# Inverting triangular blocks: four 32x32 blocks by powers and transposes, in place of two 64x64 blocks by squares

## The reference

```
h = rms_norm(x);  z = h @ w_in                      # 1024 -> q, k, v, gates of both branches
A: gated delta rule, 8 heads of 128, causal conv over 4 rows and SiLU on q, k, v
B: windowed attention, 16 heads of 64 on 2 key heads, window 128, sinks, relative bias
x + (sigmoid(gA) * (oa @ w_o_a) + sigmoid(gB) * (ob @ w_o_b)) @ w_out, then rms_norm
```

```
t_mat = eye + n_mat; p_mat = n_mat
for _ in range(5):                                  # chunks of 64
    p_mat = p_mat @ p_mat
    t_mat = t_mat + t_mat @ p_mat
```

## Time and profile before

| | |
|---|---|
| median of 3 runs | 2711.65 us |
| the profiled execution, its own time | 2707.76 us |
| its span | 2706.0 us |
| TensorE busy, matmuls | 2682.5 us, 99% |
| VectorE busy | 1416.5 us, 52% |
| ScalarE busy | 971.0 us, 36% |
| DMA, mean | 169 GB/s |

### The profile page before, as it was taken

One profiled execution on the slowest core, in us unless ns is written; L12 is line 12 of the kernel. 1 busy time (PEld: TensorE's weight loads), 2 busy tenths in 40 slices (PEclk: granted clock), 3 DMA queues, 4 the chain that ended last, 5 costly groups with the idle time before them and its releaser, 6 DMA issues.

```text
span 2706.0 us, 50329 instructions
## 1 busy us (share of the span) xinstructions
PE 2682.5 (99%) x19808; PEld 2274.0 (84%) x19808; DVE 1416.5 (52%) x3633; ACT 971.0 (36%) x3158; POOL 398.7 (15%) x238
## 2 busy tenths in 40 slices
PE   7999999999999999999999999999999999999998
PEld 6888888888888888888888888888888888888887
DVE  6777777233366666612236666651224666665012
ACT  4555455422244444421124444442112444444101
POOL 4333333443100110000000110000000011000000
PEclk9999999999999999999999999999999999999999
DMA  7554554787733333255453333335546333333564
GB/s 249 201 180 167 182 193 170 264 288 279 253 121 111 128 128 117 107 203 217 172 219 130 112 114 125 130 110 203 216 172 220 113 118 128 123 112 125 183 222 171
DMA packets 79001, 458.43 MB, mean 169 GB/s; under 512 B 13232, under 2 KB 17456, under 8 KB 31792
## 3 DMA queue, kind: packets, MB, share of 16 engines
q1 hardware_dynamic: 65664, 427.85, 44.2%
q10 hardware_dynamic: 13104, 27.36, 3.0%
HBM read 352.42 MB, written 102.76 MB: 168 GB/s over the span
## 4 chain that ended last, share of the span: by engine, by line
PE 96%; DMA 2%; POOL 1%; DVE 1%; ACT 0%; issue 0%; POOLq 0%; SPq 0%; ACTq 0%; DVEq 0%
PE bank L1305 24%; PE bank L1307 23%; PE bank L1306 23%; PE bank L1450 2%; PE last_banks L1450 2%; PE last_banks L1415 2%; PE bank L1434 2%; PE last_banks L1434 2%; PE bank L1403 2%; PE bank L1499 1%; PE bank L1491 1%; PE bank L1475 1%; PE last_banks L1557 1%; PE bank L1483 1%; PE bank L1548 1%; PE bank L1538 1%
## 5 line engine op out<-in xcount | busy, mean ns | idle before, releaser
L1305 PE MATMUL bank<-hT_hi,w_sl 128*128 128x512 f32 x2112 | 872.8, 413 | 0.0
L1307 PE MATMUL bank<-hT_hi,w_sl 128*128 128x512 f32 x2112 | 827.3, 392 | 0.0
L1306 PE MATMUL bank<-hT_lo,w_sl 128*128 128x512 f32 x2112 | 825.5, 391 | 0.0
L1307 PEld LDWEIGHTS bank<-hT_hi,w_sl 128*128 128x128 f32 x2112 | 396.7, 188 | 86.1
L1305 PEld LDWEIGHTS bank<-hT_hi,w_sl 128*128 128x128 f32 x2112 | 398.3, 189 | 71.6 <-issue 0.7
L1306 PEld LDWEIGHTS bank<-hT_lo,w_sl 128*128 128x128 f32 x2112 | 398.8, 189 | 65.4 <-issue 0.7
L436 POOL TENSOR_TENSOR w_sl<-w_raw,w_sl 128x1024 fp32r<-128x1024 f32 x90 | 218.3, 2430 | 391.2 <-ACT w_sl L517 381.6
L982 DVE SCALAR_TENSOR_TENSOR area<-zraw,stc,area 128x512 f32<-128x512 f32 x288 | 220.2, 765 | 4.2
L1148 DVE SCALAR_TENSOR_TENSOR s_cur<-s_cur,scs,last_banks 128x128 f32<-128x128 f32 x112 | 38.9, 348 | 199.8 <-PE last_banks L1554 199.8
L611 ACT ACTIVATE area<-area 128x512 f32<-128x512 f32 x96 | 60.4, 629 | 219.6 <-DVE area L982 219.6
L455 POOL TENSOR_TENSOR gu<-mk,g_hi 128x512 fp32r<-128x512 f32 x32 | 41.9, 1309 | 643.7 <-DVE nmx L1102 603.8
(11 more groups left out here) (244 smaller groups left out, 4817.7 us busy)
## 6 DMA issues: line engine op xcount, KB each, us to landing
w_sl<-saved_w SPq DMA_DIRECT2D x270, 1024.0 KB, 4.8
saved_w<-w_sl SPq DMA_DIRECT2D x90, 1024.0 KB, 4.9
w_raw<-in_w_tiles SPq DMA_DIRECT2D x90, 512.0 KB, 5.9
area<-in_x ACTq DMA_DIRECT2D x4, 2048.0 KB, 10.4
area<-in_x ACTq DMA_DIRECT2D x14, 512.0 KB, 8.1
out_y<-area ACTq DMA_DIRECT2D x3, 2048.0 KB, 8.1
bias_sb<-in_bias ACTq DMA_DIRECT2D x32, 128.0 KB, 2.3
out_y<-area SPq DMA_DIRECT2D x4, 512.0 KB, 2.7
```

The source lines that it names most:

```text
L1305: pe.matmul(dst, a_hi, b_hi, start=first, stop=False)
L1306: pe.matmul(dst, a_hi, b_lo, start=False, stop=False)
L1307: return pe.matmul(dst, a_lo, b_hi, start=False, stop=last)
```

## The change

The diagonal blocks are now of 32x32, four per tile (`BLOCKS`), and the levels are four. The stationary power is no longer made by a square on TensorE. The moving operand is the transposed power and the sum side by side (`fu_blk`, 64 columns per tile); the product gives the next transposed power, and VectorE's transpose of 32x32 blocks turns that into the next stationary power `p_blk`. There is one group of four tiles in place of two groups of two, so 16 matmuls in each apply. Behind each apply stands one fill, and the transposes of the probabilities stand behind the first. The 32x32 blocks are joined to 64x64 by two more products (`inner_in`, `inner_out`), with a copy by ScalarE between them and two by VectorE behind. The second logits are now in one piece between `inner_out` and `merge_in`. The rest of the corner is as it was. The diff, without renamed semaphores' declarations:

```diff
-LEVELS = 5
-LAST = 2 ** LEVELS
+BL = 32
+LEVELS = 4
+        BLOCKS = tuple(slice(r, r + BL) for r in range(0, P, BL))
+        CORNERS = ((BLOCKS[0], BLOCKS[1]), (BLOCKS[2], BLOCKS[3]))
-        p_sb = [blocks(area2[:, 4 * TB:4 * TB + NT * CH]), blocks(area2[:, 4 * TB + NT * CH:5 * TB])]
-        z_sb = p_sb[0]
+        z_sb = blocks(area2[:, 4 * TB:4 * TB + NT * CH])
+        inner = blocks(area2[:, 4 * TB + NT * CH:5 * TB])
+        yt, vt = inner[:, :, 0:BL], inner[:, :, BL:2 * BL]
+        f_blk, u_blk, fu_blk, p_blk = ptt[:, :, 0:BL], ptt[:, :, BL:2 * BL], ptt[:, :, 0:2 * BL], ptt[:, :, 2 * BL:3 * BL]
...
ScalarE
-                for lo, hi in HALVES:
-                    ins = act.activation(ptt[lo:hi, :, 0:CH], tt[lo:hi, :, lo:hi], ACT.Copy)
+                for r in BLOCKS:
+                    ins = act.activation(f_blk[r], tt[r, :, r], ACT.Copy)
                 ins.then_inc(pt0_ready, 1)
-                for lo, hi in HALVES:
-                    act.activation(p_sb[0][lo:hi], bch(5)[lo:hi, :, lo:hi], ACT.Copy)
...
-                for l in range(1, LEVELS + 1):
-                    p_copy(l, 0)
-                    p_copy(l, 1)
                 fill(1)
+                act.wait_ge(merge_product, merges(n1, 1))
+                act.activation(yt, bch(5)[:, :, 0:BL], ACT.Copy).then_inc(merge_act, 1)
...
VectorE
+            dve.tensor_reduce(stacked[:, :], mk[:, IDENT, :].rearrange("p (a c) -> p c a", c=BL), AX, ALU.add).then_inc(dve_init, 1)
...
-                for lo, hi in HALVES:
-                    ins = dve.tensor_tensor(ptt[lo:hi, :, CH:P], tt[lo:hi, :, lo:hi],
-                                            mk[lo:hi, IDENT:IDENT + 1, lo:hi].to_broadcast([CH, NT, CH]), ALU.add)
+                def first_powers():
+                    dve.wait_ge(pt0_ready, n1)
+                    dve.transpose(p_blk, f_blk)
+                    dve.tensor_tensor(u_blk, f_blk, stacked[:, None, :].to_broadcast([P, NT, BL]), ALU.add).then_inc(powers_ready, 1)
+                def level(l):
+                    dve.wait_ge(powers_done, powers(n1, l))
+                    dve.transpose(p_blk, bch(6)[:, :, 0:BL])
                     if l < LEVELS:
+                        ins = copy(f_blk, bch(6)[:, :, 0:BL])
                     if l > 1:
+                        dve.wait_ge(powers_ready, powers(n1, l))
+                        ins = dve.tensor_tensor(u_blk, bch(6)[:, :, BL:2 * BL], u_blk, ALU.add)
+                    ins.then_inc(powers_ready, 1)
                 def diagonal():
+                    dve.wait_ge(powers_ready, powers(n1, LEVELS + 1))
+                    dve.wait_ge(powers_done, powers(n1, LEVELS + 1))
+                    ch.link(dve.tensor_tensor(u_blk, bch(6)[:, :, BL:2 * BL], u_blk, ALU.add))
+                    dve.transpose(vt, u_blk).then_inc(merge_dve, 1)
+                    for r in BLOCKS:
+                        ins = copy(tt[r, :, r], u_blk[r])
                     ins.then_inc(diag_ready, 1)
+                def inner_corners():
+                    dve.wait_ge(merge_product, merges(n1, 2))
+                    for a, c in CORNERS:
+                        ins = copy(tt[a, :, c], bch(7)[a, :, 0:BL])
+                    ins.then_inc(merge_dve, 1)
...
                 logits(0)
+                first_powers()
                 attention()
                 fill(1)
                 quotient(0)
-                fill(2)
-                for l in range(1, LEVELS + 1):
-                    level(l, 0)
-                    level(l, 1)
-                settled()
+                fill(1)
+                level(1)
+                fill(1)
+                for l in range(2, LEVELS + 1):
+                    level(l)
                 diagonal()
+                inner_corners()
...
TensorE
+                def apply(l):
+                    c0, c1 = (0 if l <= LEVELS else BL), (2 * BL if l > 1 else BL)
+                    pe.wait_ge(powers_ready, powers(n1, l))
+                    for t in range(NT):
+                        for r in BLOCKS:
+                            ins = pe.matmul(bch(6)[r, t, c0:c1], p_blk[r, t, :], fu_blk[r, t, c0:c1], start=True, stop=True)
+                    ins.then_inc(powers_done, 1)
+                def inner_in():
+                    pe.wait_ge(merge_dve, merges(n1, 1))
+                    pe.wait_ge(merge_act, merges(n1, 1))
+                    for t in range(NT):
+                        for a, c in CORNERS:
+                            ins = pe.matmul(bch(5)[c, t, 0:BL], tt[a, t, c], vt[a, t, :], start=True, stop=True)
+                    ins.then_inc(merge_product, 1)
+                def inner_out():
+                    pe.wait_ge(merge_act, merges(n1, 2))
+                    pe.wait_ge(attn_ready, n1)
+                    for t in range(NT):
+                        for a, c in CORNERS:
+                            ins = pe.matmul(bch(7)[a, t, 0:BL], yt[c, t, :], u_blk[c, t, :], start=True, stop=True)
+                    ins.then_inc(merge_product, 1)
...
-                fill(11)
-                probs(0)
-                for l in range(1, LEVELS + 1):
-                    square(l, 0)
-                    apply(l, 0)
-                    square(l, 1)
-                    apply(l, 1)
-                    if l == 1:
-                        logits_quarters(0)
-                logits_quarters(1)
-                apply(LEVELS + 1, 0)
-                apply(LEVELS + 1, 1)
-                fill(2)
+                fill(8)
+                for l in range(1, LEVELS + 2):
+                    apply(l)
+                    fill(1)
+                    if l == 1:
+                        probs(0)
+                inner_in()
+                fill(1)
+                inner_out()
+                logits_quarters()
                 merge_in()
                 values(0)
                 merge_out()
```

More of the change, by code:

```diff
@@ L89, in state_steps, with powers, merges @@
     return (n1 - 1) * NT + t + 1 - max(0, n1 - 1 - (NB - 1) * H)
+def powers(n1, l):
+    return (n1 - 1) * (LEVELS + 1) + l
+def merges(n1, step):
+    return (n1 - 1) * 3 + step
 class Chain:
@@ L316, in build_program @@
         ft_done = sem("ft_done")
-        p0_ready = sem("p0_ready")
         pt0_ready = sem("pt0_ready")
[L319 to L324, removed]
+        powers_ready = sem("powers_ready")
+        powers_done = sem("powers_done")
         diag_ready = sem("diag_ready")
-        tz_done = sem("tz_done")
-        t11_ready = sem("t11_ready")
-        z_ready = sem("z_ready")
+        merge_product = sem("merge_product")
+        merge_act = sem("merge_act")
+        merge_dve = sem("merge_dve")
         t12_done = sem("t12_done")
@@ L689, in scaled @@
                     ins.then_inc(ready, 1)
[L691 to L694, removed]
                 squares(ssq[:, 1, :], bch(3), ssq_ready[1], 1, junk_k)
@@ L1060, in level @@
                     if l > 1:
[L1061 to L1071, removed]
@@ L1073, in diagonal @@
-                def diagonal():
[L1074 to L1080, removed]
-                    ins.then_inc(diag_ready, 1)
+                        dve.wait_ge(powers_ready, powers(n1, l))
@@ L1119, in head @@
                 quotient(0)
-                fill(2)
-                dve.wait_ge(tt0_ready, n1)
-                for l in range(1, LEVELS + 1):
-                    level(l, 0)
-                    level(l, 1)
-                settled()
+                fill(1)
[3 more added lines that the diff above has]
+                    level(l)
                 diagonal()
-                dve.wait_ge(tz_done, n1)
-                copy(z_sb[:, 0:NT // 2], bch(5)[:, 0:NT // 2, 0:CH]).then_inc(z_ready, 1)
+                inner_corners()
+                dve.wait_ge(merge_product, merges(n1, 3))
+                copy(z_sb[:, 0:NT // 2], bch(5)[:, 0:NT // 2, 0:CH]).then_inc(merge_dve, 1)
                 gated(0)
@@ L1419, in head @@
                 fill(7)
-                def square(l, g):
-                    width = CH if l < LEVELS else CH - LAST
-                    if l == 1:
-                        pe.wait_ge(p0_ready, n1)
-                        pe.wait_ge(pt0_ready, n1)
-                        pe.wait_ge(attn_ready, n1)
-                    else:
-                        pe.wait_ge(p_ready[g], n5 + l - 1)
-                        pe.wait_ge(pt_ready[g], (n1 - 1) * (LEVELS - 1) + l - 1)
-                    for t in (2 * g, 2 * g + 1):
-                        for lo, hi in HALVES:
-                            ins = pe.matmul(pv(bank[P_BANK[g]])[lo:hi, t, 0:width], ptt[lo:hi, t, 0:CH], p_sb[(l - 1) % 2][lo:hi, t, 0:width], start=True, stop=True)
-                    ins.then_inc(p_done[g], 1)
@@ L1437, in apply @@
-                def apply(l, g):
-                    c0, c1 = (0 if l < LEVELS else first_column(l)), (P if l > 1 else CH)
-                    if l == 1:
-                        pe.wait_ge(ssq_ready[0], n1)
-                    else:
```

(15 more changed lines are left out.)

35 lines of the change are left out of this document (12 added, 23 removed).

## The result

The changed kernel takes 2641.88 us (median, 2640.39 to 2643.23) against 2711.17 us for the kernel before in the same comparison: a ratio of 0.9745, interval 0.9728 to 0.9762, 69 us less. The profiled execution took 2643.21 us, with a span of 2641.3 us against 2706.0. The prediction was 2673 us with a range of 2640 to 2714: the right sign, the right bound, and a little over half of the gain. The result lies 2 us inside the range, and outside the band of 2655 to 2697 that the forecast had its chance of 0.52 for; rival C's 2633 us is nearer.

What follows compares the result with a forecast made beforehand. TensorE's own sequence was taken as the bound. Work other than fills falls from 9.89 to 8.56 us a head, 43 us over 32 heads, less 4 us of waits: 39 us, so 2673 us, range 2640 to 2714.

Steps and rivals of the forecast that it cites:

- rival C: Cheaper: half-price 32-column rounds, inner products at corner's pace, half entering and leaving; 40 us less, 2633 us; chance 0.13.
- The bound: Whole kernel: TensorE, busy 2682.5 of 2706.0 us, sets the span; other engines' work costs only where TensorE waits.
- Price of an apply: Five applies per head, 32 records each: 0.63 us each, leaving the tile mode included.
- the cheap bound: Applies 1 and 5, at 32 columns: a round may take half, 0.20 us less each.
- Price of an inner product: Two per head, 16 records at 25 ns plus 0.16 us of leaving: 0.56 us each.
- Insertions: Fills behind applies 2 to 5 and the first inner product: 0.225 us each for entering and leaving, 1.13 us.
- The waits in the levels: TensorE before the next apply: 0.04 us of wait in three levels, 0.12 a head, 4 us in all.
- Hidden work: VectorE's first-power operations and ScalarE's block copies stand where nothing waits; inner-corner copies, about 0.6 us, hide behind second logits.
- Rival A: Pace of issue: small products start no faster than 25 ns apart, 0.96 us an apply; 2726 us; chance 0.15.
- B: VectorE's chain ends last: with a transpose of 0.45 us each level waits 0.24 us longer; 2704 us; chance 0.15.
- The second logits' place: Between second inner product and corner: their 0.90 us hides VectorE's inner-corner copies; without them TensorE would wait about 0.6 us.

Runs made afterwards that it cites:

- small_split: Changed kernel with POOL's split of all weight tiles but the first three cut to 128x64 of 128x1024, the rest left out: 2626.32 us (0.9693).
- double_apply: Changed kernel with each of the five applies issued twice into the same place: 2762.98 us (1.0205).

## Why the prediction was right, and its size was not

- **The bound.** TensorE's own sequence sets the span: the later blocks gained what their array time lost, 2.5 us of 2.46. Right.
- **Price of an apply.** Right for 64 columns (0.58 for 0.63), wrong for 32: 0.38. I took the corner's pace of rounds at 64 columns for both and kept the half-price round as the cheap bound, 0.43; the value lies just below that bound. Two applies a head at 0.25 less and three at 0.05 less are 0.65 us.
- **Price of an inner product.** 0.37 for 0.56, twice: 0.38 us. The 25 ns a record of the 32-column applies before did not carry over: 16 records of 32x32 tiles, also two tiles at a time, take some 0.27 with 0.10 of leaving taken off, 17 ns each. That the size of the tiles makes the difference is likely, not shown.
- **Insertions.** 0.91 us a fill, as summed. The waits in the levels: none, for 0.12 us predicted. With small parts, 1.25 us a head more than forecast, x32 = 40 us.
- **Hidden work.** The sentence that VectorE's operations stand where nothing waits held for the later blocks, from one of which all rows had been taken. In the first block it failed: heads shorter by 2.5 us brought TensorE ahead of the loop VectorE - POOL - VectorE, and each of the 8 heads falls 1.8 us short of the gain of the others, 15 us, of which 1.46 us a head are the waits shown above. small_split gives 1.7 us a head back. This is the term that the sum lacked. The rows of the first block were to be had: ssk at 2.3 us there stood in the trace before, hidden by slack.
- **Luck in the total.** 39 + 40 - 15 = 64 us, the 64.7 of the span. The two errors have opposite signs. Without the one on the first block the time would have come out near small_split's 2626 us, below the stated range: that 2641.88 lies inside it is owed to waits that the prediction did not see.
- **Rival A**, the pace of issue, is false for single applies: 32 records in about 0.27 us are 8 to 9 ns each, and double_apply's clean heads agree, where a second set of 32 records of 32 columns adds 0.30 us (1024.99 to 1025.67, for 0.38). **B** is false by price: the transpose's start-to-start time is 0.24 us (857.29 to 857.53), for the 0.21 taken. **C** came true in part: 32-column rounds and inner products, not the entering and leaving.
- **The second logits' place** is worth what was said: 0.78 us of wait a head without it, for 0.6.

## What to carry to other kernels

Take the rows for a prediction from every stage in which the edited code runs, also where a stage has slack today: the gain stops where the next loop binds, and here one stage in four kept a quarter of it. Where a serial chain between small products can't be shortened, put other products of TensorE into each gap rather than ahead of the chain; 0.225 us of entering and leaving bought up to 0.8 us of wait and kept the clock.

## What was not expected of the hardware

- VectorE's operations with all operands in SBUF wait for POOL's running split of 128x1024 (2.36 us for 0.16; 53 of 53 in one trace), in each of the forms seen; those that read or write PSUM go on (89 of 89). Beside POOL's power on four elements an operation of 128x512 ran at its usual 0.69 us. With the splits in four pieces both engines slow down (POOL 6.47 us for 4.72, half of it without VectorE's doing; VectorE 1.13 for 0.69).
- Four 32x32 tiles on the diagonal, all writing one PSUM bank, take 32 records of 32 columns in 0.38 us and of 64 columns in 0.58, leaving included.
- Twice as many small products in a row brought 26 gaps of up to 3.9 us in which TensorE waited for no engine, each with a packet of the instruction queue close by, and 11 stretches at the lower level of the clock that begin in or right behind such gaps.
- With the fills between the levels gone, the granted clock was 0.71 in the stretch of the waits and 0.60 in the dense products behind it; in the changed kernel, with the same products and the fills between, it is 1.00 over the whole stretch.
